# Adaptive vectors of a hybrid inference step: places for the first weight blocks, a lead of two iterations for the late ones, and row sums turned by transposes

## What is computed

```
def adaln_vectors(cvec, w, b):
    m = jax.nn.silu(cvec) @ w + b
    return jnp.split(m[:, None, :], 6, axis=-1)

sh1, sc1, gt1, sh2, sc2, gt2 = adaln_vectors(cvec, W['ada_w'][l], W['ada_b'][l])
h = modulate(rms_norm(x, W['norm1_w'][l]), sh1, sc1)
y = even_mixer(h, ...)            # layer 1: odd_mixer(h, ...)
x = x + gt1 * y
h = modulate(rms_norm(x, W['norm2_w'][l]), sh2, sc2)
x = x + gt2 * sq_relu_mlp(h, W['mlp_w1'][l], W['mlp_w2'][l])
```

## Time and profile before

| | |
|---|---|
| median of 3 runs | 2430.79 us (2429.67 to 2432.89) |
| the profiled execution | 2433.58 us |
| its span | 2431.6 us |
| its TensorE clock, mean | 0.953 of full |
| busy: TensorE, VectorE, ScalarE, GpSimd | 2186.2, 1126.1, 830.7, 317.3 us |

### The profile page before, as it was taken

The page is one execution under the profiler, slowest core; times in us unless marked ns, Lnnn a source line. Parts: engine busy times, 40 slices in busy tenths (PEclk is TensorE's granted clock), DMA queues, the critical chain, the costliest instruction groups (busy, mean ns, idle before and its releaser), DMA issues. The chain is left out here.

```text
span 2431.6 us, 58582 instructions
## 1 busy us (share of the span) xinstructions
PE 2186.2 (90%) x26179; PEld 1875.3 (77%) x26179; DVE 1126.1 (46%) x2038; ACT 830.7 (34%) x1504; POOL 317.3 (13%) x542
## 2 busy tenths in 40 slices
PE   5999877878999999979996888888887889999999
PEld 3678654557999999954784767777775789999998
DVE  1242465434542343245324777777784364324421
ACT  4252353333221122143223555655653232112211
POOL 1000130001000000200001433434442100000000
PEclk7999998989999999979997999999998899999999
DMA  7211007860222222112100000000000222222221
GB/s 253 80 37 70 1 1 276 304 227 18 87 70 73 85 70 71 52 26 104 70 35 10 4 9 7 9 10 9 9 6 5 104 62 78 70 80 77 70 77 54
DMA packets 160742, 167.74 MB, mean 69 GB/s; under 512 B 13788, under 2 KB 117996, under 8 KB 160364
## 3 DMA queue, kind: packets, MB, share of 16 engines
q1 hardware_dynamic: 160492, 164.00, 20.9%
HBM read 160.44 MB, written 3.54 MB: 67 GB/s over the span
## 5 line engine op out<-in xcount | busy, mean ns | idle before, releaser
L168 PE MATMUL psum<-arena 64*64 64x64 f32 (+6 forms) x17072 | 838.0, 248 | 146.2 <-DVE arena L1952 16.2
L168 PEld LDWEIGHTS psum<-arena 64*64 64x64 f32 (+3 forms) x17072 | 668.9, 146 | 353.2 <-issue 160.7
L168 PE MATMUL psum<-hidden_high,weights_low 128*128 128x320 f32 x1024 | 233.4, 309 | 0.0
L168 PE MATMUL psum<-hidden_high,weights_high 128*128 128x320 f32 x1024 | 233.3, 309 | 0.0
L168 PE MATMUL psum<-hidden_low,weights_high 128*128 128x320 f32 x1024 | 233.2, 309 | 0.0
L638 ACT ACTIVATE weights_high<-weights 128x2048 fp32r<-128x2048 f32 x62 | 118.6, 1913 | 335.3 <-PE psum L168 335.3
L168 PE MATMUL psum<-norm_high,weights_low 128*128 128x320 f32 x992 | 226.6, 310 | 0.0
L168 PE MATMUL psum<-norm_low,weights_high 128*128 128x320 f32 x992 | 226.6, 310 | 0.0
L168 PE MATMUL psum<-norm_high,weights_high 128*128 128x320 f32 x992 | 226.5, 310 | 0.0
L701 DVE SCALAR_TENSOR_TENSOR arena<-psum,ada,arena 128x320 f32<-128x320 f32 (+2 forms) x96 | 36.3, 434 | 314.9 <-PE psum L168 314.9
L168 PEld LDWEIGHTS psum<-hidden_high,weights_high 128*128 128x128 f32 x1024 | 171.3, 188 | 0.0
(11 more groups left out here) (211 smaller groups left out, 2866.2 us busy)
## 6 DMA issues: line engine op xcount, KB each, us to landing
weights<-in_mlp_w SPq DMA_DIRECT2D x64, 1024.0 KB, 5.5
arena<-in_ada_w SPq DMA_DIRECT2D x24, 2048.0 KB, 9.4
arena<-in_ab_w_in SPq DMA_DIRECT2D x6, 2048.0 KB, 7.8
arena<-in_ab_w_out SPq DMA_DIRECT2D x2, 2048.0 KB, 9.2
arena<-in_rwkv_wv SPq DMA_DIRECT2D x2, 2048.0 KB, 7.7
arena<-in_rwkv_wr SPq DMA_DIRECT2D x2, 2048.0 KB, 8.3
arena<-in_rwkv_wk SPq DMA_DIRECT2D x2, 2048.0 KB, 7.6
arena<-in_rwkv_wo SPq DMA_DIRECT2D x2, 2048.0 KB, 10.5
```

Of the source, the lines that this page charges most:

```text
L168: return nc.tensor.matmul(out, lhsT, rhs, start=start, stop=stop, skip_group_check=shared)
```

## The change

Five edits:
1. **Places.** Blocks 2 and 3 (of `ada0`) get places of their own at unit 28, so the loads of blocks 0 to 3 wait for nothing; blocks 4 and 5 (the first two of "in") wait for the products of blocks 0 and 1. In SyncE's queue the parameter rows go ahead of all `ada_w` blocks.
2. **Late blocks.** SyncE enters `hgrn_sp` at the start of attention. TensorE does the rows of `LATE[0]` at the end of its attention stage, and in the HGRN stage, before `scores(0)`, the turn of `LATE[0]` and the rows of `LATE[1]`. Iteration m has the turn of `LATE[m+1]` and the rows of `LATE[m+2]`, so the iterations 18 and 19 have no rows and the last has no turn. Two of the pairs' outputs to HBM move to later places between the loads.
3. **Turning.** The four selection matmuls of a turn become four transposes of 128 x 128, and the four partial sums are added by one `tensor_reduce` of VectorE, straight from PSUM into `ADAS`. ScalarE's copy of the columns is gone.
4. **VectorE's order at the first norm.** The first two of the eight multiplications of `norm_scale` run ahead of the bias of the first vectors, before the end of setup.
5. **VectorE's order at HGRN's end.** `ada_dve` for the late blocks runs ahead of the last pair's `add_up` and `norm_gate`.

```diff
+        def apart(b):
+            return 2 <= b < ADA_FIRST
+        def loaded(b):
+            return S(f"apart_loaded{b % 2}" if apart(b) else f"ring_loaded{b % 2}")
         def slot(b, kt, n):
-            s = RING + (b % 2) * SLOT
+            s = 28 * T + (b % 2) * SLOT if apart(b) else RING + (b % 2) * SLOT
...
-                if b >= 2:
-                    sp.wait_ge(S("tile_product"), tiles_upto[b - 1])
+                if b >= ADA_FIRST:
+                    sp.wait_ge(S("tile_product"), tiles_upto[b - 3 if b < ADA_FIRST + 2 else b - 1])
...
             for j in range(4):
-                ins = mm(PS[:, ada_bank(l, b), 2 * j:2 * j + 2], AROWS[late(l, b)][:, b % 2, 128 * j:128 * j + 128], con(C_SEL, 2))
+                ins = nc.tensor.transpose(PS[:, ada_bank(l, b), 128 * j:128 * j + 128],
+                                          AROWS[late(l, b)][:, b % 2, 128 * j:128 * j + 128], ident)
...
-        def ada_cols_act(act, l, b):
-            act.wait_ge(S("ada_turned"), 12 * l + b + 1)
-            A.activation(ADAS[:, l, 4 * b:4 * b + 4, :].rearrange("p m g -> p (m g)"), PS[:, ada_bank(l, b), 0:8],
-                         ACT.Copy).then_inc(S("ada_cols"), 1)
+        def ada_cols(dve, l, b):
+            dve.wait_ge(S("ada_turned"), 12 * l + b + 1)
+            parts = PS[:, ada_bank(l, b), :].rearrange("p (m q x) -> p m x q", m=4, q=4)[:, :, 0:2, :]
+            V.tensor_reduce(ADAS[:, l, 4 * b:4 * b + 4, :], parts, AXX, ALU.add).then_inc(S("ada_cols"), 1)
...
         def norm_dve(dve, i):
             if i == 0:
-                norm_scale(dve, i, range(KT))
+                norm_scale(dve, i, range(2, KT))
...
             values(NA - 1)
+            ada_rows_pe(pe, *LATE[0])
...
-            return LATE[m - 1] if m else None
+            return LATE[m + 1] if m + 1 < len(LATE) else None
...
+            ada_turn_pe(pe, *LATE[0])
+            ada_rows_pe(pe, *LATE[1])
             scores(0)
...
-                ada_rows_pe(pe, *LATE[m])
+                if m + 2 < NH_:
+                    ada_rows_pe(pe, *LATE[m + 2])
...
-            ada_turn_pe(pe, *LATE[-1])
             norm(3)
...
             cumulate(0, 0, 1)
+            ada_cols(dve, *LATE[0])
             scale(0, 0, 1)
...
                 if m + 1 < NH_:
                     mask(m + 1)
+                if ada_turn_of(m) is not None:
+                    ada_cols(dve, *ada_turn_of(m))
...
+            ada_dve(dve, step, 0, ADA_FIRST, 12)
+            ada_dve(dve, step, 1, 0, 12)
             add_up(3)
             norm_gate(3)
-            ada_dve(dve, step, 0, ADA_FIRST, 12)
-            ada_dve(dve, step, 1, 0, 12)
...
             logs(0)
-            decays(0)
+            ada_act(act, *LATE[0])
+            decays(0, 0)
+            decays(0, 1)
+            ada_act(act, *LATE[1])
...
-            load_blocks(sp, "ada1", lambda i: final({7: 0, 12: 1, 18: 2}[i]) if i in (7, 12, 18) else None)
+            load_blocks(sp, "ada1", lambda i: final({9: 0, 14: 1, 18: 2}[i]) if i in (9, 14, 18) else None)
...
-            load_blocks(sp, "ada0", lambda i: load_rows(sp) if i == 0 else None)
+            load_rows(sp)
+            load_blocks(sp, "ada0")
...
-            sp.wait_ge(S("stage_done"), 4 * 3)
+            sp.wait_ge(S("stage_done"), 4 * 2)
             hgrn_sp(sp)
...
             setup_dve(dve, step)
+            for b in range(ADA_FIRST):
+                ada_cols(dve, 0, b)
+            norm_scale(dve, 0, range(2))
             ada_dve(dve, step, 0, 0, ADA_FIRST)
```

More of the change, by code:

```diff
@@ L260, in load_blocks @@
                 for x, y in parts:
-                    sp.dma_start(x, y).then_inc(S(f"ring_loaded{b % 2}"), 16)
+                    sp.dma_start(x, y).then_inc(loaded(b), 16)
                 after(i)
@@ L268, in program @@
             for blk in stages[name]:
-                per[b % 2] += 2 if isinstance(blk[0], str) else 1
-                loaded_at[b] = 16 * per[b % 2]
+                if apart(b):
+                    loaded_at[b] = 16
+                else:
+                    per[b % 2] += 2 if isinstance(blk[0], str) else 1
+                    loaded_at[b] = 16 * per[b % 2]
                 b += 1
@@ L277, in products @@
                 b = first_block[name] + i
-                pe.wait_ge(S(f"ring_loaded{b % 2}"), loaded_at[b])
+                pe.wait_ge(loaded(b), loaded_at[b])
                 w = slot(b, kt, cn)
@@ L400, in ada_rows_pe @@
             i = first_block["ada1"] + LATE.index((l, b)) if late(l, b) else first_block["ada0"] + b
-            pe.wait_ge(S(f"ring_loaded{i % 2}"), loaded_at[i])
+            pe.wait_ge(loaded(i), loaded_at[i])
             w = slot(i, 8, 512)
@@ L1216, in logs, with decays @@
                     A.activation(HT[:, d, :], h_key(p, d), ACT.Ln).then_inc(S("hgrn_log"), 1)
-            def decays(p):
-                for d in range(2):
+            def decays(p, *which):
+                for d in which:
                     act.wait_ge(S("hgrn_cum"), 2 * p + d + 1)
@@ L1254, in hgrn_act @@
                     key_rows(m + 1)
-                if ada_turn_of(m) is not None:
-                    ada_cols_act(act, *ada_turn_of(m))
                 if i == 0 and p < 3:
@@ L1259, in hgrn_act @@
                 if i == 2 and p < 3:
-                    decays(p + 1)
+                    decays(p + 1, 0, 1)
                 out(m)
-                ada_act(act, *LATE[m])
+                if m + 2 < NH_:
+                    ada_act(act, *LATE[m + 2])
                 if i == 0 and p:
@@ L1266, in hgrn_act @@
                     rms(p - 1)
-            ada_cols_act(act, *LATE[-1])
             square(3)
@@ L2335, in _ @@
                 ada_act(act, 0, b)
-                if b:
-                    ada_cols_act(act, 0, b - 1)
                 if b == 1:
@@ L2340, in _ @@
                     norm_rms(act, step, 0)
-            ada_cols_act(act, 0, ADA_FIRST - 1)
             stage_end(act, "act")
```

## The result

| | before | changed |
|---|---|---|
| median | 2430.34 us (4 runs, 2429.67 to 2432.89) | 2403.99 us (4 runs, 2402.47 to 2404.98) |
| ratio | | 0.9889, 95% interval 0.9871 to 0.9907 |
| profiled execution, span | 2433.58, 2431.6 us | 2404.98, 2403.0 us |
| TensorE clock, mean | 0.953 | 0.959 |

In a second series the changed kernel's ratio was 0.9895 (0.9878 to 0.9912). Executions of one kernel lie up to 13 us apart (60 of the kernel before: 2420.9 to 2433.8), and the longer ones are mostly those with the lower mean clock. So a single trace tells where time goes, and the ratios of whole series tell how much.

A forecast was written before the change was run, and what follows sets the result against it. Outside the gaps time was taken as TensorE's, with setup waiting for two loads. Setup's 10.5 us plus HGRN's 9.1 (tail 10.1 less 1.0 for head and loop) gave 19.6, so a median of 2411.2 us, range 2404 to 2422.

The forecast's parts named there:

- Setup, 10.5 forecast: Setup up to the first product of "in": loads without idle slices and earlier parameters gain 11.1 us, taken as 10.5.
- The stall of the first small row: SyncE's queue in setup: a 5.93 us issue, should it recur, lands block 3 at up to 40, gain 8.6 us.
- Head, +2.7 forecast: HGRN before the loop: added rows and reduction start it 2.05 us later, iteration 0's turn adds 0.66; together +2.7.
- The loop, 1.7 of 5.4 forecast: HGRN's iterations: shorter turns save at most 5.4 us, but mostly lengthen waits for loads, leaving 1.7.
- The tail, 10.1 forecast: HGRN's end: 10.3 us behind the last states in place of 20.4, a gain of 10.1.
- The rule on the clock: HGRN's turns: selection matmuls and transposes run at either clock level; by the skill's rule full clock may not come with transposes.
- My fourth: Rival: the loop gets all 5.4 us of the turns and the clock stays high, 2406 us; chance 0.13.
- The second: Rival: SyncE's queue stalls in setup, gain there 4 us, HGRN 9, 2418 us; chance 0.18 with the only-setup-gains rival.
- third: Rival: HGRN's loop falls to 1.2 GHz, some 9 us an iteration, up to 2473 us; chance 0.05.
- The first: Rival: only setup gains, 10.5 us, HGRN 2 as its loop waits for loads, 2418; chance 0.18 with the setup-stall rival.

The follow-up runs named there:

- setup undone: Changed kernel with setup's loads in their old order and places and all eight first-norm multiplications behind the stage's end: median 2413.9 us, ratio 0.9944.
- the kernel with selection: Changed kernel with four selection matmuls and VectorE's copy in place of transposes and reduction: median 2412.9 us, ratio 0.9930.
- the four traces with the changed program: Traces with the changed kernel's TensorE program in HGRN: changed (2403.99 us), changed again (2405.7), setup's edits undone (2413.9), late bias behind the last norm again (2405.9).
- old places: Changed kernel with late blocks at their old places, loads asked for after attention, late bias at the end: 2407.0 us, ratio 0.9911.
- half loads: Changed kernel loading only four of eight k tiles of each late block: 2398.0 us, ratio 0.9882; with selection matmuls 2409.2, 0.9926.
- the kernel with two selection matmuls: Changed kernel with half of each late block loaded and only two of four selection matmuls per late turn: median 2400.3 us, ratio 0.9876.

## Why the prediction was off

Its direction was right, and so were its mechanisms for setup, for the waits for loads and for the tail. Its size was too small: 19.6 us for 26.4, with the result a hundredth of a microsecond outside the range. The term that failed is edit 3, the loop's 1.7 us, worked out without the clock. By its steps:

- **Setup, 10.5 forecast.** 11.3 in the trace, 10.1 between the second traces of both kernels (54.85 and 44.80), 12 to 13 by the ratio with setup undone. The step-by-step sum of 11.1 was right almost throughout: rows of block 2 at 35.1 (34.6 forecast) and of block 3 at 38.0 (37.5), "in" at 45.3 (45.5). The stall of the first small row didn't recur. Of this, 1.0 us is the shorter turns.
- **Head, +2.7 forecast.** `scores(0)` came 1.65 later instead of 2.05. From there to the first rows it became 2.0 shorter instead of 0.66 longer in the first trace. I took the old spacing, which held half clock for `scores` to `outputs` (1.23, 1.86, 2.32 us), as if it were the work's length, and didn't price what a filled head might do. But the other three traces of the same program have 8.0 to 9.2 us there, for the 9.0 that my terms give. So the 3.0 us that the head came out better in the first trace are mostly luck.
- **The loop, 1.7 of 5.4 forecast: the step that failed.** I argued that shorter turns only wait longer for loads. They do: the waits rose by 2.7 us (8.0 less 5.3), and by 3 to 4 against the kernel with selection. But the step left out the clock. The loop took 110.3 to 115.7 us in the four traces with the changed program, 113.3 on average, for 117.0 and 117.3 before and 117.3 with selection: 4 us saved for 1.7. With transposes the excess was 8.0 and 12.6 in the changed kernel's two traces, for 12.7 and 14.3 before. Edit 3 as a whole measured 9.7 us alone and some 9 in company, of which 1.0 lies in setup and, alone, 5.2 in the old tail. In company the traces place only some 5 of the 9.
- **The tail, 10.1 forecast.** 10.4 in the trace (10.1 left for 20.5), close to what was worked out; only the norm's product took 2.50 us for 2.2. But the old tail held 5 us that the transposes also take away (15.2 and 15.3 us with old places), so edits 2 and 5 measure only 4 to 5 us beside them (0.9889 and 0.9895 against 0.9911), and 7.4 were booked for head and tail.
- **The rule on the clock.** I weighed it as a danger only. The Trainium skill ("TensorE: Matmul & The Clock Gate", Part 4: PE-mode transpose) says that full clock doesn't engage for transposes, since they don't count as busy in the same way. By it the transposes should have cost clock, and this wasn't measured: edit 3 alone was 9.7 us faster, and with half loads four and eight transposes a turn went with 7.3 and 7.9 us of excess, for 11.3 with selection. Among matmuls, transposes ran at full clock (four in 0.60 us, eight in 1.04). So the measurement decides against the rule in this setting, and I had no rival with its sign turned.
- **The rivals.** My fourth, "more than forecast", with 2406, was the nearest, and its reason (more of the turns' saving, clock higher) the nearest to what was measured, though it gave the clock's gain to the filled head and not to edit 3; I gave it 0.13. The second (setup stalls) and third (clock falls) are refuted. The first is half true: the loop does wait for loads.

Open is why the clock is higher with edit 3, and how much of it is the kind of instruction. The timed series give edit 3 some 2 to 3 us beyond the turns' length (9.7 less 1.0 in setup and 10.7 less 0.7, against 6.7), no more than their intervals of 3 to 5 us; the kernel with two selection matmuls puts it at nothing.

## What to carry to other kernels

Before the length of a group is used in a sum, compare it with the shortest group of the same shape: if it is longer, it holds a half clock that the change may move, and that belongs in the sum with both signs. Two edits that shorten the same tail aren't additive; price each on the kernel that already has the other. When a step is replaced by a cheaper one on TensorE, ask also what the new instructions do for the clock, and measure several executions, since two traces of the same kernel can differ by 5 us in one stage. Before one trace is used in an argument, compare its time with the median of its series.

## What was not expected of the hardware

- Selection matmuls of 128 stationary and 2 moving columns (0.95 us for eight instructions) went with more time at 1.2 GHz than transposes or identity matmuls with 128 moving columns: excess 11 us against 7 to 8 with half loads. It is one trace of each, and four traces of one program differ by more (5.4 to 12.6), so this is a hint and not a finding.
- The mean clock of the same kernel varies from execution to execution (0.950 to 0.954 over the eleven executions of the kernel before in one series), and its time with it, 2433.3 us at 0.950 and 2425.2 at 0.954. The same TensorE program had 5.4 to 12.6 us of excess in a stage of 140 to 145 us.
- A small DMA of 48 KB took 5.93 us to issue behind 5.7 MB in the queue (5.79 to 6.13 in three other traces), and 0.67 us behind 3.7 MB (0.60 and 0.61 in two others).
